# Two channel LayerNorms of a decoder step: sums collected tile by tile, statistics on 88 rows, products in thirds

## What is computed

```
z = x @ w_in + b_in
u, conv_state = causal_dwconv(conv_prev, a * sigmoid(g), conv_dw_w, conv_dw_b)      # 31 taps
y_conv = silu(layer_norm(u, conv_ln_g, conv_ln_b)) @ w_conv_out
...                                                                                  # latent attention
mix = (g_conv * y_conv + g_mla * y_mla) @ w_mix_out
x1 = layer_norm(DN_ALPHA * x + mix, ln1_g, ln1_b)
h, ffn_state = causal_dwconv(ffn_prev, x1 @ w_up, ffn_dw_w, ffn_dw_b)
f = (silu(hg) * hv) @ w_down
y = layer_norm(DN_ALPHA * x1 + f, ln2_g, ln2_b)
```

## Time and profile before

| | us |
|---|---|
| median of 3 runs (2285.85 to 2295.95) | 2294.15 |
| the profiled execution | 2278.77 |
| its span, first to last instruction | 2276.9 |
| TensorE busy, share of the span | 2101.8, 92% |
| VectorE busy | 1324.0, 58% |
| ScalarE busy | 654.0, 29% |
| GpSimd busy | 443.0, 19% |
| mean granted TensorE clock | 0.953 of full |

### The profile page before, as it was taken

One profiled execution on the slowest core, in us unless ns is written; L12 is line 12 of the kernel. 1 busy time (PEld: TensorE's weight loads), 2 busy tenths in 40 slices (PEclk: granted clock), 3 DMA queues, 4 the chain that ended last, 5 costly groups with the idle time before them and its releaser, 6 DMA issues.

```text
span 2276.9 us, 34903 instructions
## 1 busy us (share of the span) xinstructions
PE 2101.8 (92%) x13705; PEld 1989.7 (87%) x13705; DVE 1324.0 (58%) x1743; ACT 654.0 (29%) x1066; POOL 443.0 (19%) x230
## 2 busy tenths in 40 slices
PE   5999999969989999979989996799999999999992
PEld 5999999958979888866659995699999999999992
DVE  4799999964536666634433324855444454454545
ACT  3221222135224444433422102522222222222212
POOL 2222221101100010033311221121221222212213
PEclk6999999989979999989988997899999999999995
DMA  7222222215310000045624431011111111111102
GB/s 222 66 60 72 75 65 66 85 46 176 124 41 13 12 23 12 19 187 222 260 107 132 122 102 47 19 56 38 52 46 40 46 37 56 47 37 47 46 27 99
DMA packets 161092, 173.64 MB, mean 76 GB/s; under 512 B 19564, under 2 KB 136102, under 8 KB 156852
## 3 DMA queue, kind: packets, MB, share of 16 engines
q1 hardware_dynamic: 142805, 97.63, 14.6%
q0 software_dynamic: 8368, 46.27, 5.3%
q10 hardware_dynamic: 9825, 28.48, 3.4%
HBM read 145.48 MB, written 27.73 MB: 76 GB/s over the span
## 4 chain that ended last, share of the span: by engine, by line
PE 68%; issue 15%; DVE 12%; ACT 3%; DMA 1%; ACTq 1%; POOL 0%; DVEq 0%; POOLq 0%; SPq 0%
PE psb L1753 18%; PE psa L1753 18%; PE psb L2188 6%; PE psa L2188 6%; PE psb L1862 5%; PE psa L1862 4%; DVE pst L1262 4%; PE psb L2088 1%; PE pst L2067 1%; DMA xt_d<-xst 1%; PE psa L2035 1%; PE psb L2035 1%; PE pst L1932 1%; DVE ptl L1411 1%; PE psb L1767 1%
## 5 line engine op out<-in xcount | busy, mean ns | idle before, releaser
L1262 DVE SCALAR_TENSOR_TENSOR pst<-g_ext,wtap,pst 128x512 f32<-128x512 f32 x464 | 306.9, 745 | 0.0
L1179 POOL TENSOR_TENSOR wlo<-wraw,whi 128x1024 fp32r<-128x1024 f32 x64 | 173.3, 2720 | 637.8 <-ACT whi L1046 637.8
L1643 DVE TENSOR_SCALAR hg<-ueg,fwv,vec 128x1024 f32<-128x1024 f32 x22 | 17.9, 813 | 231.1 <-ACT ueg L1063 231.1
L1115 POOL TENSOR_TENSOR wlo<-wraw,whi 128x1024 fp32r<-128x1024 f32 x32 | 77.0, 2412 | 377.6 <-ACT whi L648 358.3
L1753 PE MATMUL psa<-x1h,whi 128*128 128x352 f32 x528 | 115.9, 328 | 18.2 <-DVE x1l L1618 16.6
L1121 POOL TENSOR_TENSOR wlo<-wraw,whi 128x1024 fp32r<-128x1024 f32 x32 | 77.3, 2417 | 270.4 <-ACT whi L682 270.3
L1753 PE MATMUL psa<-x1h,wlo 128*128 128x352 f32 x528 | 114.2, 324 | 0.0
L1753 PE MATMUL psb<-x1h,whi 128*128 128x352 f32 x528 | 114.2, 324 | 0.0
L1753 PE MATMUL psa<-x1l,whi 128*128 128x352 f32 x528 | 114.1, 324 | 0.0
L1753 PE MATMUL psb<-x1h,wlo 128*128 128x352 f32 x528 | 113.8, 323 | 0.0
L1753 PE MATMUL psb<-x1l,whi 128*128 128x352 f32 x528 | 113.7, 323 | 0.0
(11 more groups left out here) (423 smaller groups left out, 5245.2 us busy)
## 6 DMA issues: line engine op xcount, KB each, us to landing
wraw<-in_w_up SPq DMA_DIRECT2D x44, 512.0 KB, 3.7
wraw<-in_w_in SPq DMA_DIRECT2D x37, 512.0 KB, 3.8
wraw<-in_w_down SPq DMA_DIRECT2D x22, 512.0 KB, 3.5
gb_d<-stg ACTq DMA_DIRECT2D x8, 528.0 KB, 2.7
ga_d<-stg ACTq DMA_DIRECT2D x8, 528.0 KB, 2.7
gab<-ga_d ACTq DMA_DIRECT2D x8, 528.0 KB, 4.4
ma_d<-stg ACTq DMA_DIRECT2D x8, 528.0 KB, 2.9
tmp<-gb_d SPq DMA_DIRECT2D x8, 528.0 KB, 3.7
```

What stands on the lines that cost most here:

```text
L1115: nc.gpsimd.tensor_tensor(wlo[:, n % HL, :], wraw[:, n % RAW, :], whi[:, n % HL, :].bitcast(F32), ALU.subtract).then_inc(lo_done, 1)
L1179: nc.gpsimd.tensor_tensor(wlo[:, (ns + 2) % HL, :], wraw[:, (ns + 2) % RAW, :], whi[:, (ns + 2) % HL, :].bitcast(F32), ALU.subtract).then_ ...
L1262: half[x] = link(nc.vector.scalar_tensor_tensor(out=dst, in0=src, scalar=tap(k_), in1=pst[:, x, :], op0=ALU.mult, op1=ALU.add))
```

## The change

Both norms get their statistics from data that are centred by a provisional value: the mean over the first two channel blocks (`ones` matmul, scale 1/256), the same for all later blocks. It is subtracted from each block as it comes; sums and sums of squares run along. The true mean and variance then come from 24 or 16 small matmuls with one moving column (`token_sums`), which put 88 tokens on partitions, so that mean, variance, root and reciprocal work on 88 x 12 or 88 x 4 numbers. `spread` brings 1/sigma and -mean/sigma back to all partitions by products with the identity. Each block gets a multiplication and an addition in place of one multiplication.

In the convolution the provisional sum stands after block 3 (CSUM); GpSimd centres blocks 0 to 6 and adds them and their squares, ScalarE squares between its stage-1 reads, VectorE does block 7. The conv-state rows are transposed and written out later, in one piece. In LN1 VectorE does all of it; mix6 and mix7 are made in thirds with the sums and spreads of a third between them, and so is the first pair of FFN products (`first_up`). The ALPHA scalings of the residual move behind the first FFN convolutions. The ACT and GpSimd loops of stage 1 are written out. New names: d centred, p sum, sq square, q sum of squares, y scaled input less the provisional mean, br spread copied, u n normalised, x h affine and high part, l low part.

```diff
+                    if t == 2 and m >= CSUM:
+                        for k in ((0, 1) if m == CSUM else (m - 2,)):
+                            square(k)
+                if m == CSUM - 1:
+                    act.wait_ge(cl_p, 1)
+                    nc.scalar.activation(split(stat[:, :]), acc(0), ACT.Copy, scale=1.0 / (2 * P)).then_inc(free[0], 1)
...
+                swish(m)
+                if m == 2:
+                    read_z("q0", 3, 1, V_Q)
+                if m == 5:
+                    read_z("q1", 4, 0, V_Q + 1)
+                    act.wait_ge(keep_tr, 1)
+                    for r in range(2):
+                        nc.scalar.activation(krow[:, r * 512:(r + 1) * 512], pst[0:KEEP, r, :], ACT.Copy).then_inc(keep_rd, 1)
+                    act.wait_ge(keep_rd, 2)
+                    act.dma_start(O["conv_p"][0, 0], krow[0:HALO, :]).then_inc(krow_out, 16)
+                    for b in range(NB):
+                        act.dma_start(O["conv_s"][0, b, HALO - NT:, :], krow[HALO + b * NT:HALO + (b + 1) * NT, :]
+                                      ).then_inc(krow_out, 16)
+            read_z("q2", 5, 1, V_Q + 2)
 
...
+            for m in range(2, 6):
+                hi(N4 + m + 3)
+                mixed(m)
+                act.wait_ge(l1_v, VS[f"q{m - 1}"])
+                step(f"sq{m}", nc.scalar.activation(tmp[0][:, :], res[:, m, :], ACT.Square))
...
+            hi(N5 + 1)
+            square(6, 0)
+            square(7, 0)
+            sums_root(0)
+            square(6, 1)
+            spread(0)
+            affine(0, 0)
+            affine(0, 1)
+            square(7, 1)
+            affine(0, 2)
+            affine(0, 3)
+            sums_root(1)
+            square(6, 2)
+            spread(1)
+            affine(0, 4)
+            square(7, 2)
+            affine(0, 5)
+            affine(0, 6)
+            affine(0, 7)
+            sums_root(2)
+            affine(1, 0)
+            affine(1, 1)
+            spread(2)
...
+            for k in range(2, MT):
+                affine(1, k)
+            for kind in (GATE0, VAL0):
+                ffn_hi("first", kind)
+            for k in range(MT):
+                affine(2, k)
...
+            def centre(m):
+                pool.wait_ge(conv_chain, STEPS * (m + 1))
+                pool.wait_ge(free[0], U1A[0] + 2 * CSUM + 2)
+                step(f"d{m}", nc.gpsimd.tensor_tensor(u[:, m, :], u[:, m, :], stat[:, :], ALU.subtract))
+                if m:
+                    pool.wait_ge(cl_g, CG[f"d{m}"])
+                    first = u[:, 0, :] if m == 1 else s1[:, :]
+                    step(f"p{m}", nc.gpsimd.tensor_tensor(s1[:, :], first, u[:, m, :], ALU.add))
+
+            def add_squares(m):
+                pool.wait_ge(cl_s, CS[f"sq{m}"])
+                step(f"q{m}", nc.gpsimd.tensor_tensor(tmp[1][:, :], tmp[1][:, :], tmp[0][:, :], ALU.add))
...
+                if m >= CSUM:
+                    for k in ((0, 1) if m == CSUM else (m - 2,)):
+                        centre(k)
+                lo(4 * m + 2)
+                lo(4 * m + 3)
+                if m >= CSUM:
+                    add_squares(max(1, m - 2))
+            lo(N1B)
...
+            step("d", nc.vector.tensor_tensor(u[:, MT - 1, :], u[:, MT - 1, :], stat[:, :], ALU.subtract))
+            dve.wait_ge(cl_v, CV["d"])
+            dve.wait_ge(cl_g, CG[f"q{MT - 2}"])
+            step("p", nc.vector.tensor_tensor(s1[:, :], s1[:, :], u[:, MT - 1, :], ALU.add))
+            dve.wait_ge(cl_s, CS[f"sq{MT - 1}"])
+            step("q", nc.vector.tensor_tensor(tmp[1][:, :], tmp[1][:, :], tmp[0][:, :], ALU.add))
...
+                    step(f"u{m}", nc.vector.tensor_tensor(u[:, m, :], u[:, m, :], stat[:, :], ALU.mult))
+                    dve.wait_ge(cl_v, CV[f"u{m}"])
+                    step(f"n{m}", nc.vector.tensor_tensor(u[:, m, :], u[:, m, :], s1[:, :], ALU.add))
...
+            dve.wait_ge(l1_s, AS["c2"])
+            shifted(2)
+            shifted(3)
...
+            for m in range(2, 6):
+                q, n = ring[f"mix{m}"]
+                dve.wait_ge(w_used, N4 + m + HL + 1)
+                dve.wait_ge(l1_v, VS[f"y{m}"])
+                nc.vector.tensor_tensor(split(res[:, m, :]), split(stg[m % 2][:, :]), acc(q), ALU.add).then_inc(free[q], 1)
+                mixed(m)
+                step(f"p{m}", nc.vector.tensor_tensor(s1[:, :], s1[:, :], res[:, m, :], ALU.add))
+                dve.wait_ge(l1_s, AS[f"sq{m}"])
+                step(f"q{m}", nc.vector.tensor_tensor(tmp[1][:, :], tmp[1][:, :], tmp[0][:, :], ALU.add))
+                shifted(m + 2)
...
+            last_mix(6, 0)
+            add_sums(0)
+            last_mix(7, 0)
+            variance(0)
+            scales(0)
+            last_mix(6, 1)
+            add_sums(1)
+            normalise(0, 0)
+            normalise(0, 1)
+            last_mix(7, 1)
+            normalise(0, 2)
+            normalise(0, 3)
+            variance(1)
+            scales(1)
+            last_mix(6, 2)
+            add_sums(2)
+            normalise(0, 4)
+            last_mix(7, 2)
+            normalise(0, 5)
+            normalise(0, 6)
+            for k in range(6):
+                low(0, k)
+            normalise(0, 7)
+            variance(2)
+            low(0, 6)
+            low(0, 7)
+            scales(2)
+            for c in (1, 2):
+                for k in range(MT):
+                    normalise(c, k)
+                    if k:
+                        low(c, k - 1)
+                low(c, MT - 1)
+
+            def scale_residual(ms):
...
+            pe.wait_ge(conv_chain, 2 * STEPS)
+            for c in range(3):
+                for m in range(2):
+                    last = nc.tensor.matmul(psx[0][:, c, 0:CH], ones[:, :], u[:, m, c * CH:(c + 1) * CH],
+                                            start=m == 0, stop=m == 1)
+            last.then_inc(cl_p, 1)
...
+            pe.wait_ge(cl_v, CV["q"])
+            for kind, src in enumerate((s1, tmp[1])):
+                for x in range(3 * SUB):
+                    last = nc.tensor.matmul(pst[0:ST, 0, 480 + kind * 3 * SUB + x:481 + kind * 3 * SUB + x],
+                                            src[:, x * ST:(x + 1) * ST], ones[:, 0:1], start=True, stop=True)
...
+                if k in (2, 4, 6):
+                    spread(k // 2 - 1)
...
+            def token_sums(c):
+                pe.wait_ge(l1_v, VS[f"q6{c}"])
+                pe.wait_ge(l1_s, AS[f"sq7{c}"])
+                if c == 0:
+                    pe.wait_ge(pf_r, 2)
+                else:
+                    pe.wait_ge(l1_s, AS[f"br{c - 1}"])
+                if c == 2:
+                    q, n = ring["mix7"]
+                    pe.wait_ge(free[q], n + 2)
+                for kind, parts in enumerate(((s1[:, :], res[:, 7, :]), (tmp[1][:, :], stg[1][:, :]))):
+                    for x in range(SUB):
+                        cols = slice(c * CH + x * ST, c * CH + (x + 1) * ST)
+                        for k, src in enumerate(parts):
+                            last = nc.tensor.matmul(pst[0:ST, 0, 480 + kind * SUB + x:481 + kind * SUB + x], src[:, cols],
+                                                    ones[:, 0:1], start=k == 0, stop=k == 1)
+                step(f"t{c}", last)
...
+            for m in range(6):
                 weighed(N4 + m, f"mix{m}", mgh, mgl, ml_done if m == 0 else None)
...
+                if m == 2:
+                    shift_sum()
+                if m == 3:
+                    state_rows()
...
+            between = {(6, 1): (token_sums, 0), (7, 1): (spread, 0), (6, 2): (token_sums, 1), (7, 2): (spread, 1)}
+            for c in range(3):
+                for m in (6, 7):
+                    if c == 0:
+                        pe.wait_ge(lo_done, N4 + m + RAW + 1)
+                        ready(f"mix{m}")
+                    j = ring[f"mix{m}"][0]
+                    third(N4 + m, j, c, mgh, mgl, range(0, 3))
+                    if (m, c) in between:
+                        what, of = between[(m, c)]
+                        what(of)
+                    last = third(N4 + m, j, c, mgh, mgl, range(3, KT))
+                    if c < 2:
+                        step(f"m{m}{c}", last)
+                    else:
...
+            def first_up():
+                for c in range(3):
+                    for v, kind in enumerate((GATE0, VAL0)):
+                        n, ns = blk("first", kind)
+                        wh, wl = slot3(whi, ns), slot3(wlo, ns)
+                        if c == 0:
+                            pe.wait_ge(lo_done, n + (RAW + 1))
+                            pe.wait_ge(free[v], acc5("first", kind, v) + 1)
+                        out = psx[v][:, c, 0:CH]
+                        for k in range(KT):
+                            if v == 0:
+                                pe.wait_ge(l1_s, AS[f"h{c}{k}"])
+                            for w in (wh, wl):
```

(11 more changed lines are left out.)

532 lines of the change are left out of this document (342 added, 190 removed).

## The result

| | us |
|---|---|
| the change, median | 2298.0 |
| the kernel before beside it, median | 2292.4 |
| ratio, 95% interval | 1.0031 (1.0020 to 1.0041) |
| the change, profiled execution, and its span | 2294.82, 2293.0 |
| granted TensorE clock, mean | 0.964 |

The change makes the kernel slower by 0.2 to 0.4%. I had forecast 2287.2, 0.3% faster: inside the range and inside "no change" as I had bounded it, but on the other side of zero. The loss is 5.6 us by the medians and 7 by the ratio. One execution of the change among 20 took 4180.95 us and doesn't count in the ratio; no run explains it.

The account below looks back on a forecast made before the run. TensorE's waits at the two LayerNorms were taken as the bound, at most 87 us to win. A convolution gain of 14.3 and LN1 loss of 7.3 gave 2271.8 profiled, plus 15.4 a median of 2287.2; range 2266 to 2304.

Parts of the forecast that it names:

- Convolution norm, up to kr and from kr: Convolution norm's two stretches: kr ends at 458.8, q0 at 481, and the latent sums start at 534.9 instead of 549.4.
- Gain 14.3: Convolution norm as a whole: 14.3 us won by the start of the latent sums, bounds 9 and 19.
- LN1, up to mix7: Mix products: a circle of 12.1 us a round against TensorE's 11.65, mix7 waits 3.9 us, token sums start at 1398.9.
- LN1, from there: First token sums to first value product's end: last sums end at 1430.3, the product at 1475 instead of 1467.5.
- A loss of 7.3 us: LN1 to the first value product's end: 7.3 us lost, bounds a gain of 5 and a loss of 14.
- (d): Rival, chance 0.11: half clock from the wait at mix7 lasts to the value product's end; 2319, or 2307 if it returns.
- Behind them, cost at nothing: After LN1: residual scalings between the first FFN steps cost nothing; attention and the rest of the FFN as before.
- Sum: Whole kernel: -14.3 + 7.3 = -7.0 us on the profiled execution, 2278.77 to 2271.8.
- From the profiled execution to the median: Whole kernel: the median lies 15.4 us above the profiled execution, as before, giving 2287.2 us.
- (a): Rival, chance 0.49: the kernel's net effect stays within 0.5%, as worked out.
- (b): Rival, chance 0.28: LN1's split misses the add, rounds of 10.9 us, clock holds; 19 to 24 us faster, 2273.
- (c): Rival, chance 0.09: weights land under 5 us after the read, little idle before LN1's token sums; 33 us won, 2261.

Follow-up runs that it names:

- q2_earlier: Against splits_late, ScalarE reads q2 and converts ya1's weights before the seventh swish, reloads z before the eighth, issues the nine output DMAs later: 2251.5 us, 0.9893 to before.
- ln1_only: The kernel before with only the change's LN1 parts, the convolution norm as before: 2306.3 us, ratio 1.0062 to before.
- squares_ahead_of_ffn_weights: The change with ScalarE's squares ahead of the conversions of mix weights and of the first FFN weights: 2284.2 us, ratio 0.9969 to before.
- splits_late: squares_ahead_of_ffn_weights with the last spread's read behind six affine steps and the second gate and value weight conversions behind the last affine step: 2273.6 us, 0.9931 to before.
- before_shift_141: The kernel before with 141 more already fulfilled waits in TensorE's program ahead of the FFN loop: 2284.6 us, ratio 1.0042 to before.

## Why the prediction was wrong

- **Convolution norm, up to kr and from kr**: right, within 2 us at every mark. "The latent sums start at 534.9" was 1.3 us early: the reload was issued sooner (520.8 for 522.1) but landed 12.7 us later, for 10.4 before, and the `gab` load behind it had the last word, where I had priced two squares. **Gain 14.3** measured 13 at that mark and 10 to 12 behind it. The missing term is the half clock in the sums, 3.1 us: I had looked for idle stretches of TensorE only in LN1. Here too it stood still for 4.7 us. q2_earlier took both away.
- **LN1, up to mix7**: the mechanism was right in every joint, and two edits that break it give 11 and 12 us back. The forecast wait at mix7 was 3.9 us and measured 3.3. The first token sums came 2.2 us late against the same clock, because the last load took 6.07 us instead of 5.0 and the second split held the scaled input (3.39 instead of 1.25).
- **LN1, from there**: this is the step that failed, by size. "A loss of 7.3 us" measured 11.4 (ln1_only 14), inside the bound of 14. The marks slip by 2.2 us at the first token sums and by 4.6 at the last (1430.3 forecast, 1434.9). The mis-sized term is the thirds of product between the first and the last token sums: 3.6 of them, 14 us at the full clock that I took, measured 17.6. Behind the first sums 15 matmuls took 4.61 us for 2.44, behind the second 3.81. I had put half clock only where TensorE stands idle, and squares_ahead_of_ffn_weights and splits_late show it behind narrow sums after waits of 1.3 and 1.1 us as well. A row that I had cited says so too: of the 8 us at clock 0.50 from 1195 on TensorE is busy for 7.11, and my sentence that the trace has this level only beside long idle stretches was wrong. The two splits of 2.4 us, the spread ahead of the affine steps and the last third at 1.43 a tile all stood where I had put them.
- **A slip in the working**: three spreads and five thirds, as named there, would put the end of the last sums at 1437.9. The 1430.3 comes out with the two spreads and 3.6 thirds that lie ahead of it, as rival (d) counts them.
- **Behind them, cost at nothing**: it costs 1 to 3 us. The FFN loop lies elsewhere in TensorE's program and now stands idle at all four back edges (3.7 us for 1.7 and 3.3 in the two profiles before), which before_shift_141 brings about in the kernel before by place alone.
- **Sum**: three misses of 3, 4 and 1 us with one sign, on a sum of -7.0, make +1, and the pair of profiles shows +0.7. The medians are 5.6 us apart. The other 5 us stand in no profile, and their cause stays open; that the clock in LN1 differs between executions would fit, and isn't shown. Each term lay in its bounds; a small difference of two large terms doesn't give a sign.
- **From the profiled execution to the median**: I added 15.4 us as a constant. Some 13 us of it are the rounds of the sample attention, most likely on another kind of chip. That the constant came near for the median is luck of which chips were drawn; read from the two profiles alone, the change would seem to lose 16 us.
- **The rivals**: (a) is what happened by its number, 0.31%, though the sign is the other one. (b) assumed no collisions, and all were there. (c) needed loads under 5 us; they took 4.7 to 6.1. (d) did not happen as a lasting level: the clock came back at 1412, in the second third of mix7, but four stretches of 3.4 to 10.2 us at half clock followed. The rule of the Trainium skill that gaps throttle the clock (TensorE: Matmul & The Clock Gate, section HAM oscillation) agrees with three stretches here, 0.57, 0.50 and 0.50, each behind an idle one of 3.3 to 8.6 us; my sum went by it in one place of three. It doesn't account for the stretches behind narrow transposes and sums, at 1354.3 and 1422.6, and there the measurement decides.
- What the prediction did not see at all is how near the better kernel was. The thirds and the sums on 88 rows gain 10 to 16 us in LN1 once a few entries of ScalarE's queue stand elsewhere.

## What to carry to other kernels

When a step is made to run along with a product, write down the round that it forms through all queues, weight loads and conversions too, and compare it with the product's time: here 12.1 to 13 us against 11.65 led to waits that cost about 12 us, and one swap on ScalarE's queue removed them. Filling an idle stretch of TensorE with narrow products is not free either: here wide products behind them ran at half clock, so price what follows at both levels. On an in-order queue put what the next product's operands need ahead of what is only needed later, and splits on GpSimd where VectorE has a pause. Before two profiles are compared, look for a stretch that neither kernel changed; if it differs, the executions are no partners.

## What the runs showed of the hardware

- The same loop of the sample attention took 21.0 us a round on two chips of the experiments and 23.4 on two others, 12.6 to 14 us over six rounds, with TensorE idle among transposes that wait for nothing visible.
- Wide products ran at clock 0.50 behind 44 transposes of 16 columns without a gap (1354.3 to 1357.7 in the change), and 15 of them took 4.03 and 4.61 us instead of 2.44 behind sums of one moving column after waits of 1.1 and 1.3 us.
- 141 instructions that do nothing, put ahead of the FFN loop, raised the packets on the instruction queue from 59 and 68 to 86 and made each of four turns start with an idle time of 0.7 to 1.1 us. The Trainium skill (Runtime: NRT & Kernel Launch, section Instruction fetch mechanics) says that a branch whose target has left the loaded window stalls until the page is fetched; the packets and the idle times at the back edges agree. Which place is good no run here shows; counting within 16 KB did not tell it.
- With GpSimd's split running, two VectorE subtractions took 3.33 and 3.34 instead of 1.2 us in the convolution norm, 2.59 instead of 1.26 in LN1, and even steps of 352 columns 2.64 and 2.60 instead of about 0.5.
